# A hybrid decoder step on one core: the 16 learned rows moved into the sequences' tile, and 320 instead of 336 rows behind the keys

## The chip, the cores and the metric

The kernel runs on 1 core of one Trainium2 chip. The metric is the device time of one execution in microseconds. An execution was also profiled: its trace gives each instruction's engine, source line, start and duration. Engines are written as the profile writes them: PE is TensorE's matmul, PEld its weight load, DVE is VectorE, ACT is ScalarE, POOL is GpSimd, SP is SyncE; L723 is line 723 of the kernel.

## The reference

One layer is computed for two kinds of sequences: a prompt of 256 rows, ahead of which 16 learned rows stand (272 positions), and 8 running sequences with 8 new rows each (64 rows) and 1024 cached positions. Width is 1024, all in fp32.

```python
u = rmsnorm(h, norm1_g) @ w_in
z, xbc, dt_raw, q, k, v, f_raw, gate_s, gate_a = split(u)
xbc = silu(causal_dwconv(concat(conv_prev, xbc), conv_w, conv_b))      # width 4
y, ssm_state = ssm_run(xs, dt, A, Bm, Cm)                              # chunks: 16 learned rows, then 128 and 128
y = grouped_rmsnorm((y + d_skip * xs) * silu(z), ssd_norm_g)
o = attn_run(q, k, v, logf)              # causal; logit = q.k / 8 + c_q - c_k, c the running sum of log forget
mix = sigmoid(gate_s) * (y @ w_ssd_br) + sigmoid(gate_a) * (o @ w_attn_br)
h = h + mix @ w_out
h = h + hier_moe(rmsnorm(h, norm2_g))    # 4 groups x 8 experts, top 1 group, top 2 experts in it
y_prompt = rmsnorm(hp, final_norm_g)[:, 16:]
```

Returned are the outputs of the 256 prompt rows and of the 64 sample rows, the keys, values and log forget values of all 272 and 64 rows, the state-space states and the last convolution rows. The outputs of the 16 learned rows are not returned; their keys, values, log forget values, convolution rows and their part of the state are needed by the rows behind them.

## The kernel before

The 336 rows lie in three tiles, `ROWS = [128, 128, 80]`, beginning at columns 0, 128 and 256 of the transposed activations `xnT`. Tile 0 holds the 16 learned rows and prompt rows 0 to 111, tile 1 prompt rows 112 to 239, and tile 2 (80 rows) the 64 sample rows and then prompt rows 240 to 255. Each fp32 matmul shows as two records in the trace. The phases follow one another; each is a block with one instruction stream for each engine, and ends in a barrier.

*Setup.* The rows are normed and transposed, keys, values, time steps and forget values of all 336 rows are computed, and running sums are taken as products with triangular matrices (`tri_le`, `tri_le2` for tile 2, `ones` and `tailrow` for totals); `c_q` and `ncT` are those of log forget. POOL writes the masks `mask_d` (128 x 256) and `mask_t` (for the last 16 query rows).

*State-space phase.* Eight groups of 4 heads. For each, PE projects 512 channels over all 336 columns (`channels`, L667, 64 records), ACT and VectorE do the convolution and SiLU, then `chunks` does the rest: z gates (L676), transposes to rows (L688), decay products (L698), transposes of the old states (L709), products of states (L718), outputs inside a chunk (L723), outputs from the incoming state (L727, L733, L736), and new states of the samples (L751). Then PE goes on with the channels of the next group, as soon as VectorE has added up the first half of the samples' states (L645), which frees the PSUM banks. The order on VectorE behind the products of states is fixed by the program: copy of the first state L608, then decay (L611) and sum (L615) for the second and third; then the output rows of tile 0, 1, 2 (L621 to L631); then the prompt's state out (L637), and the samples' states (L639, L645). Tile 0 starts from a zero state, so it has two operations (L621, L631), while tiles 1 and 2 have four (L623, L627, L629, L631). POOL scales x by time step, end decay and skip for tile 0, 1, 2 (L503, three products each), and then spreads B over the samples (L506). The product of states of a tile waits for POOL's products of that tile:

```python
for t, r in enumerate(ROWS):
    pe.wait_ge(x_ok, 3 * g + t + 1)
    k0 = 64 if t == 2 else 0
    o = ps[7][:, 256 * t:256 * t + 256] if t < 2 else ps[3][:, 0:256]
    pe.matmul(o, tok[k0:r, t, 256:384], xw[k0:r, t, :], start=True, stop=True).then_inc(st_ps, 1)
```

*Attention, prompt.* Eight passes, each for a pair of heads. `scores` (L1103) has three products a head, for query tiles of 128, 128 and 16 rows over 128, 256 and 336 keys; then PE computes q of the next pair over all 336 columns (`project_q`, L1091, 16 records), while VectorE adds decay and mask (L1020), takes maxima (L1025), and after ScalarE's exponentials (L945) the reciprocal (L1031) and the scaling (L1036). Then PE transposes the weights (L1110 to L1115, six a head), ScalarE copies them out (L949, L950), and PE multiplies with v (L1122). The weights of q have one buffer `w_q`: POOL issues the two transfers for the next pair in `load_wq` (L868) once the projection that reads them is done (`q_ps`).

*Attention, samples*: one sequence after another over cached pages.

*Merge.* Eight column tiles: two gates (L1344), the state-space branch (L1349) and the attention branch (L1352), 40 products of 336 columns each; then the output product row tile by row tile (L1360), norm, transposes and router.

*Route, experts, final.* Each of the 336 rows chooses two experts; the pairs are counted into blocks of 64 rows, each block of one expert. For each block SP streams 6 MB of weights (`w_gate_up` in three buffers, `w_down` in two), PE gathers the rows with a 0/1 product over the three row tiles (L1700), and the block is computed (L1722, L1737). In the end the rows' two results are gathered, added and normed, and sent.

## Time and profile before

| what | value |
|---|---|
| runs of the kernel | 1520.16, 1515.48, 1518.97 us, median 1518.97 |
| profiled execution | 1519.67 us, its span 1518.0 us, mean granted clock 0.932 of 2.4 GHz |
| PE / PEld busy | 1338.1 us (88%) / 740.9 us (49%) |
| DVE / ACT / POOL busy | 493.4 us (32%) / 263.9 us (17%) / 207.1 us (14%) |
| setup | 0 to 78 us |
| state-space phase | 78 to 482 us |
| attention, prompt (loop of eight pairs) | 482 to 602 us (from 495) |
| attention, samples | 602 to 733 us |
| merge, output product and router | 733 to 919 us, 919 to 979 us |
| route | 979 to 1000 us |
| experts | 1000 to 1489 us |
| final | 1489 to 1518 us |

The stages' limits are read from the first and last instruction of their lines. A share of busy time is an average over stages with different limits: PE's 88% has the experts' phase in it, where DMA runs at 0.94. In an order of time each row has start (us), duration (us; of several merged instructions from the first start to the last end), engine, line, operation, tiles and count, and in brackets how long the engine stood idle before it and what ended that.

### The profile page before, as it was taken

The numbers are of one execution on the slowest core, as the hardware profiler recorded it, in microseconds if no ns is written. First come the engines' busy times: TensorE is split into PE (matmuls) and PEld (weight loads), VectorE is DVE, ScalarE is ACT, GpSimd is POOL, SyncE is SP. The second block draws the span as 40 slices with busy tenths as digits, with TensorE's granted clock in tenths as the row PEclk, the third lists the DMA queues.
The fourth block names the chain that finished last, engine by engine and source line by source line (L and its number), as shares of the span: only waits on it lengthen the run. The fifth ranks groups of instructions, "written<-read, shape, count | busy, mean of one in ns | idle before, by whom it ended". The sixth has DMA issues, their size and how long they took to land. (4 is left out here: it accounts for less than half of the span.)

```text
span 1518.0 us, 19560 instructions
## 1 busy us (share of the span) xinstructions
PE 1338.1 (88%) x6097; PEld 740.9 (49%) x6097; DVE 493.4 (32%) x1106; ACT 263.9 (17%) x677; POOL 207.1 (14%) x401
## 2 busy tenths in 40 slices
PE   5899999999995898877799999669999999999990
PEld 3666667666763455645566664423333333333330
DVE  2236654556456465333000001331221212122123
ACT  1122233223322344222000000001010111101011
POOL 3023443244324111010000000100000000000003
PEclk9789999989997898999899999779999999999995
DMA  6033324422422227543865370169999999999974
GB/s 195 19 111 88 113 83 142 114 86 83 142 59 58 45 52 250 176 149 104 247 145 120 87 235 0 69 284 421 429 428 429 429 429 429 429 428 429 428 295 128
DMA packets 171554, 318.30 MB, mean 210 GB/s; under 512 B 21147, under 2 KB 148563, under 8 KB 159235
## 3 DMA queue, kind: packets, MB, share of 16 engines
q1 hardware_dynamic: 162610, 302.03, 54.8%
q10 hardware_dynamic: 6864, 8.94, 1.7%
q0 software_dynamic: 2048, 6.95, 1.6%
q8 instruction: 16, 0.26, 0.1%
q14 instruction: 16, 0.12, 0.0%
HBM read 289.20 MB, written 28.68 MB: 209 GB/s over the span
## 5 line engine op out<-in xcount | busy, mean ns | idle before, releaser
L667 PE MATMUL psg<-stretch 128*128 128x336 f32 x512 | 162.3, 482 | 11.3 <-DVE h_sample_out L645 9.6
L1722 PE MATMUL ph<-w_gate_up,x_gathered 128*64 128x512 f32 x704 | 162.2, 612 | 0.9 <-DVE x_gathered L1670 0.9
L667 PEld LDWEIGHTS psg<-stretch 128*128 128x128 f32 x512 | 105.0, 207 | 70.4 <-DVE h_sample_out L645 15.4
L1737 PE MATMUL py<-w_down,h_t 128*64 128x512 f32 x512 | 116.9, 598 | 3.5 <-DMA w_down<-in_w_exp_down 3.4
L1682 DVE SCALAR_TENSOR_TENSOR h_gate<-h_tanh,ph 128x256 f32<-128x256 f32 x32 | 13.5, 421 | 301.0 <-ACT h_tanh L1639 301.0
L1722 PEld LDWEIGHTS ph<-w_gate_up,x_gathered 128*64 128x64 f32 x704 | 49.4, 135 | 108.5 <-issue 108.5
L1700 PE MATMUL px<-yT,block_rows 128*64 128x512 f32 (+1 forms) x396 | 92.9, 605 | 10.7 <-DVE block_rows L1665 10.7
L582 DVE SCALAR_TENSOR_TENSOR x_conv<-x_padded,conv_wh,x_conv 128x360 f32<-128x360 f32 x96 | 57.0, 594 | 103.5 <-ACT x_conv L531 92.6
L676 PE MATMUL psg<-stretch 128*128 128x256 f32 (+1 forms) x384 | 84.5, 380 | 0.0
L1344 PE MATMUL psm<-stretch,w_merge 128*128 128x336 f32 x256 | 76.2, 457 | 6.9 <-DMA w_merge<-in_w_in 6.9
L1774 POOL DMA_INDIRECT y_expert<-expert_rows,slot_i x6 | 6.2, 1041 | 510.2 <-PEq L1744 508.7
L676 PEld LDWEIGHTS psg<-stretch 128*128 128x128 f32 (+1 forms) x384 | 67.3, 177 | 14.5
L1722 PE MATMUL ph<-stretch,x_gathered 128*64 128x512 f32 x320 | 73.9, 612 | 0.0
L1349 PE MATMUL psm<-yT,w_merge 128*128 128x336 f32 x256 | 73.6, 446 | 0.0
L1344 PEld LDWEIGHTS psm<-stretch,w_merge 128*128 128x128 f32 x256 | 49.9, 196 | 31.7 <-issue 9.0
L1304 DVE SCALAR_TENSOR_TENSOR mix_part<-gate_tanh,psm 128x336 f32<-128x336 f32 x16 | 7.4, 501 | 178.5 <-PE psm L1352 178.5
L1737 PEld LDWEIGHTS py<-w_down,h_t 128*64 128x64 f32 x512 | 33.9, 136 | 64.2 <-issue 58.9
L1700 PEld LDWEIGHTS px<-yT,block_rows 128*64 128x64 f32 (+1 forms) x396 | 28.3, 139 | 70.0 <-issue 59.2
L1349 PEld LDWEIGHTS psm<-yT,w_merge 128*128 128x128 f32 x256 | 48.6, 190 | 23.7
L1091 PE MATMUL psa<-stretch,w_q 128*128 128x336 f32 x128 | 42.3, 488 | 16.1 <-DVE k_and_c L1000 12.6
L1639 ACT ACTIVATE h_tanh<-ph 128x256 f32<-128x256 f32 x32 | 12.3, 384 | 211.4 <-PE ph L1722 211.4
L1722 PEld LDWEIGHTS ph<-stretch,x_gathered 128*64 128x64 f32 x320 | 22.4, 135 | 49.3 <-issue 49.3
(414 smaller groups left out, 1791.1 us busy)
## 6 DMA issues: line engine op xcount, KB each, us to landing
w_down<-in_w_exp_down SPq DMA_DIRECT2D x32, 2048.0 KB, 19.6
w_gate_up<-in_w_exp_gate SPq DMA_DIRECT2D x22, 2048.0 KB, 17.0
w_gate_up<-in_w_exp_up SPq DMA_DIRECT2D x22, 2048.0 KB, 21.4
stretch<-in_w_exp_gate SPq DMA_DIRECT2D x10, 2048.0 KB, 18.7
stretch<-in_w_exp_up SPq DMA_DIRECT2D x10, 2048.0 KB, 23.1
stretch<-in_w_in SPq DMA_DIRECT2D x16, 1024.0 KB, 5.1
stretch<-in_w_in SPq DMA_DIRECT2D x16, 512.0 KB, 7.4
h<-in_state_ssm SPq DMA_DIRECT2D x16, 512.0 KB, 4.9
```

What stands on the lines that cost most here:

```text
L582: i = v.scalar_tensor_tensor(xc[:, m, :], xp[:, m, w:w + 360], S["conv_wh"][:, w, bass.ds(o, 1)], xc[:, m, :], ALU.mult, ALU.add)
L667: mm = pe.matmul(ps[m][:, 0:T], wg[:, k, P * m:P * m + P], S["xnT"][:, k, :], start=(k == 0), stop=(k == KT - 1))
L676: mm = pe.matmul(ps[4 + t // 2][0:r, 256 * (t % 2):256 * (t % 2) + 256], S["xnT"][:, k, COL[t]:COL[t] + r], wg[:, k, 512:768], start=(k == ...
L1091: mm = pe.matmul(ps[0][:, 0:T], wq[:, k, :, :], S["xnT"][:, k, :], start=(k == 0), stop=(k == KT - 1))
L1304: k = v.scalar_tensor_tensor(mx_[h][:, j, :], th[h][:, j, :], 1.0, ps[4 * h + 2 + j][:, 0:T], ALU.add, ALU.mult)
L1344: mm = pe.matmul(ps[4 * h + j][:, 0:T], wm[h][:, 8 * j + k, :], S["xnT"][:, k, :], start=(k == 0), stop=(k == KT - 1))
L1349: pe.matmul(ps[4 * h + 2][:, 0:T], wm[h][:, 16 + k, :], S["yT"][:, k, :], start=(k == 0), stop=(k == 15))
L1639: act.activation(th[:, :], ph[:, 0:256], ACT.Tanh, scale=0.5).then_inc(th_ok, 1)
L1682: v.scalar_tensor_tensor(hg[:, :], th[:, :], 1.0, ph[:, 0:256], ALU.add, ALU.mult).then_inc(gu_free, 1)
L1700: mm = pe.matmul(px[64 * j:64 * j + 64, :], sel[0:r, t, :], S["hn"][0:r, t, 512 * j:512 * j + 512], start=(t == 0), stop=(t == 2))
L1722: mm = pe.matmul(ph[64 * j:64 * j + 64, :], xg[:, k % 4, k // 4, :], w_gu[w][:, :, k, :].rearrange("p g (q c) -> p g q c", c=4)[:, :, :, 2 ...
L1737: mm = pe.matmul(py[h][64 * j:64 * j + 64, :], ht[:, k % 2, k // 2, :], w_dn[h][:, k, 512 * j:512 * j + 512], start=(k == 0), stop=(k == 3))
```

## The change

The learned rows move from the front of tile 0 to the end of tile 2 (columns 320 to 335). Tiles 0 and 1 now hold the 256 prompt rows, and tile 2 the 64 sample rows and the 16 learned rows. What needs all 336 rows (norm, channels, keys, values, time steps, running sums, states) runs as before on `ROWS`; what only the returned outputs need runs on `QROWS = [128, 128, 64]` and `TQ = 320` columns: z gates, y, q, gates, branches, output product, norm, router, experts and final norm. The first chunk of the scan is now the 16 rows of tile 2, and tiles 0 and 1 both start from a state. Keys are laid out with the 16 learned ones first (`k_and_c`, 272 columns), so there are two query tiles with 144 and 272 keys, and the learned rows' v is copied to `v_meta`. The numbers of expert blocks that the program provides for (`NBLK` 42, `LEAST_BLK` 10) come out as before; one of the five comparisons that count an expert's blocks falls away. The diff, cut to its core:

```diff
+TQ = SEQ + NS
+QROWS = [128, 128, 64]
-            sp.dma_start(S["xtok"][0:16, 0, :], A["meta_tokens"]).then_inc(x_in, 16)
-            sp.dma_start(S["xtok"][16:128, 0, :], xp[0:112, :]).then_inc(x_in, 16)
-            sp.dma_start(S["xtok"][:, 1, :], xp[112:240, :]).then_inc(x_in, 16)
+            sp.dma_start(S["xtok"][:, 0, :], xp[0:128, :]).then_inc(x_in, 16)
+            sp.dma_start(S["xtok"][:, 1, :], xp[128:256, :]).then_inc(x_in, 16)
...
-            sp.dma_start(S["xtok"][64:80, 2, :], xp[240:256, :]).then_inc(x_in, 16)
+            sp.dma_start(S["xtok"][64:80, 2, :], A["meta_tokens"]).then_inc(x_in, 16)
...
-            pool.memset(S["mask_t"][:, :], 0.0)
             pool.drain()
-            keep(S["mask_d"][:, 128:256], [[-1, P]], 0, 1, fill=NEG)
-            pool.memset(S["mask_t"][:, 256:320], NEG)
-            keep(S["mask_t"][:, 320:336], [[-1, 16]], 0, 1, fill=NEG)
+            keep(S["mask_d"][:, 144:272], [[-1, P]], 0, 1, fill=NEG)
...
-            pe.matmul(o[:, 128:144], S["tri_le"][:, :], lf[:, 0, :], start=True, stop=True)
-            pe.matmul(o[:, 144:160], S["ones"][:, :], lf[:, 0, :], start=True, stop=False)
+            pe.matmul(o[:, 128:144], S["tailrow"][:, :], lf[0:80, 2, :], start=True, stop=False)
+            pe.matmul(o[:, 128:144], S["tri_le"][:, :], lf[:, 0, :], start=False, stop=True)
+            pe.matmul(o[:, 144:160], S["tailrow"][:, :], lf[0:80, 2, :], start=True, stop=False)
+            pe.matmul(o[:, 144:160], S["ones"][:, :], lf[:, 0, :], start=False, stop=False)
             pe.matmul(o[:, 144:160], S["tri_le"][:, :], lf[:, 1, :], start=False, stop=True)
-            pe.matmul(o[0:16, 160:176], S["ones"][:, 0:16], lf[:, 0, :], start=True, stop=False)
-            pe.matmul(o[0:16, 160:176], S["ones"][:, 0:16], lf[:, 1, :], start=False, stop=False)
-            pe.matmul(o[0:16, 160:176], S["tri_le2"][:, 64:80], lf[0:80, 2, :], start=False, stop=True)
...
-                for t, r in enumerate(ROWS):
-                    v.wait_ge(y_ps, 3 * g + t + 1)
-                    if t == 0:
-                        v.tensor_tensor(y[0:r, t, :], ps[4 + t][0:r, 0:256], dx[0:r, t, :], ALU.add)
-                    else:
-                        v.tensor_tensor(yo[0:r, t, :].rearrange("k (h p) -> k h p", h=4),
...
+                for t, r in enumerate(QROWS):
+                    v.wait_ge(y_ps, 3 * g + t + 1)
+                    v.tensor_tensor(yo[0:r, t, :].rearrange("k (h p) -> k h p", h=4),
+                                    ps[4 + t][0:r, 256:512].rearrange("k (h p) -> k h p", h=4),
+                                    bc(S["eac"][0:r, t, bass.ds(4 * g, 4)].unsqueeze(2), [r, 4, HP]), ALU.mult)
+                    v.drain()
+                    v.tensor_tensor(y[0:r, t, :], ps[4 + t][0:r, 0:256], yo[0:r, t, :], ALU.add)
+                    v.drain()
+                    v.tensor_tensor(y[0:r, t, :], y[0:r, t, :], dx[0:r, t, :], ALU.add)
...
-                for t, r in enumerate(ROWS):
-                    pe.wait_ge(x_ok, 3 * g + t + 1)
-                    k0 = 64 if t == 2 else 0
-                    o = ps[7][:, 256 * t:256 * t + 256] if t < 2 else ps[3][:, 0:256]
-                    pe.matmul(o, tok[k0:r, t, 256:384], xw[k0:r, t, :], start=True, stop=True).then_inc(st_ps, 1)
+                pe.wait_ge(x_ok, 3 * g + 3)
+                for t in (2, 0, 1):
+                    k = slice(64, 80) if t == 2 else slice(0, P)
+                    o = (ps[7][:, 256:512], ps[3][:, 0:256], ps[7][:, 0:256])[t]
+                    pe.matmul(o, tok[k, t, 256:384], xw[k, t, :], start=True, stop=True).then_inc(st_ps, 1)
...
-                    if t == 1:
-                        pe.wait_ge(hp_ok, 3 * g + 1)
-                        mm = pe.matmul(ps[5][:, 256:512], xs[:, 3, P:2 * P], hp[:, 0, :], start=True, stop=True)
+                    if t < 2:
+                        pe.wait_ge(hp_ok, 3 * g + t + 1)
+                        mm = pe.matmul(ps[4 + t][:, 256:512], xs[:, 3, 16 + P * t:16 + P * t + P], hp[:, t, :],
+                                       start=True, stop=True)
                     if t == 2:
                         pe.wait_ge(compact, 2 * g + 2)
-                        pe.wait_ge(hp_ok, 3 * g + 2)
                         pe.wait_ge(ht_ev, 4 * g + 4)
-                        pe.matmul(ps[6][64:80, 256:512], cx[:, 8, 64:80], hp[:, 1, :], start=True, stop=True)
...
-        keys = [128, 256, T]
-        qrows = [128, 128, TAIL]
+        keys = [144, 272]
...
-                    for c in range(3):
-                        k = 3 * g2 + c
-                        r = qrows[c]
-                        act.wait_ge(nm_ok, 6 * t + k + 1)
+                    for c in range(2):
+                        k = 2 * g2 + c
+                        act.wait_ge(nm_ok, 4 * t + k + 1)
...
-                    act.activation(pt[:, g2, 0:416], ps[5 + 2 * g2][:, 0:416], ACT.Copy)
-                    act.activation(pt[0:80, g2, 416:432], ps[5 + 2 * g2][0:80, 416:432], ACT.Copy).then_inc(pt_ev, 1)
+                    act.activation(pt[:, g2, :], ps[5 + 2 * g2][:, 0:384], ACT.Copy)
+                    act.activation(ptm[:, g2, :], ps[2 + 2 * g2][0:16, 0:256], ACT.Copy).then_inc(pt_ev, 1)
...
-                    mm = pe.matmul(ps[0][:, 0:T], wq[:, k, :, :], S["xnT"][:, k, :], start=(k == 0),
+                    mm = pe.matmul(ps[0][:, 0:TQ], wq[:, k, :, :], S["xnT"][:, k, 0:TQ], start=(k == 0),
...
+                    for c in range(2):
+                        pe.transpose(bm_[0:16, P * c:P * c + P], sc[:, g2, c, 0:16], idn[:, :])
+                        pe.transpose(b[:, P * c:P * c + P], sc[:, g2, c, 16:144], idn[:, :])
+                    pe.transpose(b[:, 256:384], sc[:, g2, 1, 144:272], idn[:, :]).then_inc(pt_ps, 1)
...
+                for g2 in range(2):
+                    pe.matmul(ps[6][64 * g2:64 * g2 + 64, 0:256], S["v"][:, 0, P * u + HD * g2:P * u + HD * g2 + HD],
+                              pt[:, g2, 0:256], start=True, stop=False)
+                for g2 in range(2):
+                    pe.matmul(ps[6][64 * g2:64 * g2 + 64, 128:256], S["v"][:, 1, P * u + HD * g2:P * u + HD * g2 + HD],
+                              pt[:, g2, 256:384], start=False, stop=False)
+                for g2 in range(2):
+                    mm = pe.matmul(ps[6][64 * g2:64 * g2 + 64, 0:256],
+                                   vm[:, P * u + HD * g2:P * u + HD * g2 + HD], ptm[:, g2, :],
+                                   start=False, stop=True)
...
-                            mm = pe.matmul(ps[4 * h + j][:, 0:T], wm[h][:, 8 * j + k, :], S["xnT"][:, k, :],
+                            mm = pe.matmul(ps[4 * h + j][:, 0:TQ], wm[h][:, 8 * j + k, :], S["xnT"][:, k, 0:TQ],
...
-                for t, r in enumerate(ROWS):
+                for t, r in enumerate(QROWS):
```

The last pair of lines stands for all the loops over row tiles from the z gates on.

## Rows read from the trace of the kernel before

**Rows 1.** Busy us by stage: PE, PEld, DVE, ACT, POOL; PEclk, DMA share, GB/s.
```profile
...
78.00:482.00 404.00, 381.26 (x1725) 263.62 (x1726) 219.91 (x376) 118.00 (x304) 145.20 (x283) 0.94 0.34 98
...
495.00:602.00 107.00, 92.45 (x416) 54.28 (x416) 63.11 (x225) 43.71 (x158) 17.64 (x20) 0.91 0.38 103
...
733.00:919.00 186.00, 183.56 (x640) 122.90 (x640) 11.38 (x24) 7.22 (x16) 0.00 (x0) 0.98 0.62 164
...
1000.00:1489.00 489.00, 469.13 (x2128) 157.94 (x2128) 95.88 (x228) 51.12 (x97) 0.00 (x0) 0.99 0.94 399
```

**Rows 2.** Order of time, tail of one state-space group: start, duration, engine, line.
```profile
...
262.78 1.03 PE L718 MATMUL psg<-x_wend,x_b_rows 128*128 128x256 f32 x4
...
263.84 0.42 DVE L608 COPY h_prompt<-psg 128x256 f32<-128x256 f32 x1 [0.79 <-PE psg L718]
...
264.47 0.48 DVE L611 TENSOR_TENSOR h_prompt<-h_prompt,dec 128x256 f32<-128x256 f32 x1 [0.20 <-issue]
264.63 2.07 POOL L506 TENSOR_TENSOR b_by_seq<-x_b_rows,seg 64x1024 f32<-64x1024 f32 x1
...
264.71 0.69 PE L718 MATMUL psg<-x_wend,x_b_rows 16*128 16x256 f32 x2 [0.91 <-POOL x_skip L503]
...
265.64 1.34 DVE L611 TENSOR_TENSOR h_prompt<-h_prompt,dec 128x256 f32<-128x256 f32 x1 [0.20 <-PE psg L718]
...
267.56 0.42 DVE L621 TENSOR_TENSOR y_rows<-psg,x_skip 128x256 f32<-128x256 f32 x1
...
268.41 0.42 DVE L623 TENSOR_TENSOR y_off<-psg,eac 128x256 f32<-128x256 f32 x1
...
272.21 0.41 DVE L637 COPY h_prompt_out<-psg 128x256 f32<-128x256 f32 x1
...
275.17 1.49 PE L667 MATMUL psg<-stretch 128*128 128x336 f32 x2 [1.37 <-DVE h_sample_out L645]
```

**Rows 3.** Order of time in the attention loop: one middle pair, the sixth, the last.
```profile
...
516.79 1.75 POOL L868 DMA_DIRECT2D w_q<-in_w_in  x2 [11.67 <-PE psa L1091]
...
519.34 2.44 PE L1103 MATMUL psa<-k_and_c,q_pad 128*128 128x128 f32 x10
...
522.38 4.79 PE L1091 MATMUL psa<-stretch,w_q 128*128 128x336 f32 x16
...
527.00 0.27 PE L1110 MATMUL psa_s<-ident,scores 128*128 128x128 f32 x1
...
580.96 2.25 PE L1091 MATMUL psa<-stretch,w_q 128*128 128x336 f32 x7 [0.63 <-DMA w_q<-in_w_in]
...
596.58 0.47 PE L1110 MATMUL psa_s<-ident,scores 128*128 128x128 f32 x1 [4.29 <-DVE scores L1036]
```

**Rows 4.** Order of time on PE, two ends of another group.
```profile
...
311.39 1.03 PE L718 MATMUL psg<-x_wend,x_b_rows 128*128 128x256 f32 x4
...
326.61 21.35 PE L667 MATMUL psg<-stretch 128*128 128x336 f32 x64 [1.37 <-DVE h_sample_out L645]
```

**Rows 5.** Windows of 6 us, columns as in rows 1; PEclk is the granted clock.
```profile
...
214.00:220.00 6.00, 5.75 (x36) 4.50 (x38) 5.21 (x10) 0.51 (x2) 3.19 (x4) 0.72 0.00 0
...
274.00:280.00 6.00, 4.83 (x12) 3.18 (x13) 5.70 (x8) 0.00 (x0) 4.85 (x8) 0.72 0.00 0
...
316.00:322.00 6.00, 6.00 (x31) 3.27 (x30) 2.85 (x8) 1.02 (x4) 1.48 (x4) 0.50 0.00 0
```

**Rows 6.** Groups of instructions by line and shape, the third query tile on VectorE.
```profile
...
L1025 DVE TENSOR_REDUCE neg_max<-scores 16x1 f32<-16x336 f32 x16 | 7.7, 480 | 0.0
...
L1036 DVE TENSOR_SCALAR scores<-scores,row_sum 16x336 f32<-16x336 f32 x16 | 6.0, 376 | 0.0
...
L1020 DVE SCALAR_TENSOR_TENSOR scores<-psa_s,c_q,mask_t 16x336 f32<-16x336 f32 x8 | 4.4, 546 | 0.0
```

**Rows 7.** DMA issues of the attention stage: KB each, median us to landing.
```profile
...
w_q<-in_w_in POOLq DMA_DIRECT2D x16, 256.0 KB, 4.0
```

**Rows 8.** Order of time in setup, one pair of wide products.
```profile
...
71.82 0.59 PE L350 MATMUL ps<-lf,tri_le 128*128 128x16 f32 x2
```

240 lines of the change are left out of this document (107 added, 133 removed).

## The prediction

> **What bounds the kernel now.** I read the busy time by stage first [rows 1]. The stages follow one another, each ended by a barrier, so a stage that shortens or lengthens moves all that follows. The last long one, the experts, keeps the DMA engines at 0.94 of their time while it streams weights: its length is that of its bytes, and fewer rows shorten it only if a 64-row block disappears. The routing worked out from the reference's inputs gives each of the 32 experts 10 to 33 pairs with the 16 learned rows and 10 to 31 without them. So there are 32 blocks before and 32 after, and the stage keeps its length; a block less would have been worth about 6 MB at 399 GB/s, 16 us. That leaves the three stages before it, and each has its own bound.
>
> In the state-space stage TensorE is busy 381 of 404 us. The order of time in one of the eight groups [rows 2] shows where it isn't: it waits 0.91 us for POOL's products of the third tile (L718), and 1.37 us at the head of the next group's L667 for VectorE's L645. From L608 to L645 VectorE runs almost without a hole, and TensorE's wait hangs on its end. Whatever lengthens that chain lengthens the group.
>
> In the prompt's attention the order of time of one head pair [rows 3] shows scores (L1103), then the next pair's q projection (L1091), then the transposes (L1110) as soon as the projection ends: TensorE goes from one to the next, and VectorE's softmax lies beneath the projection. Only the last pair has no projection, and there L1110 waits 4.29 us for VectorE.
>
> In the merge TensorE is busy 183.6 of 186 us with 640 records of 336 columns [rows 1].
>
> **The change part by part.**
>
> *Merge.* All 640 records go from 336 to 320 columns. In proportion that is 183.6 x 16/336 = 8.7 us off a stage in which nothing else waits. The output product, the transposes and the router behind it stream the same number of columns: nothing.
>
> *State-space stage, the waits.* The first product of states is now that of the learned rows, which lie in the third tile, so all three L718 pairs wait for POOL's last product. The first of them starts at 264.71 instead of 262.78. The 16-row pair lasts until 265.34 (the next line's start is taken as that: 264.71 plus 0.63, an estimate from the pair's 0.69); the pair behind it ends 0.6 later, the four records' 1.03 less two steps of 0.21. VectorE's copy L608 then starts near 265.97, not at 263.84: 2.13 later. Some comes back: the second L611 took 1.34 against 0.48 for the first, beside POOL's L506 (264.63 plus 2.07 is 266.70, and the long one ends 0.28 after that). Started 2 us later, both multiplications fall at or behind 266.6: 0.86 back.
>
> *State-space stage, the work.* The first tile gets the term of the starting state: two VectorE instructions and a product more. The first tile's two operations take 268.41 - 267.56 = 0.85, the two other tiles' four each take 272.21 - 268.41 = 3.80, 1.90 a tile. Three tiles of four are 5.70 against 4.65: 1.05 more. TensorE's added product lies beneath this chain, as does the one taken out (L733) and POOL's saved copy; the 80-row operations that become 64-row ones have as many elements per partition and cost the same.
> Together 2.13 - 0.86 + 1.05 = 2.3 us a group, 8 groups, 18.6 us. Bounds: 1.05 x 8 = 8.4 if the later start were hidden, (2.13 + 1.05) x 8 = 25.4 if nothing comes back.
>
> *State-space stage, the clock.* TensorE's wait at L718 grows from 0.91 us to about 1.8, the one at L667 from 1.37 to 3.7. After the 1.37 us wait the granted clock falls in each group (0.72 in the mean of 274 to 280 us [rows 5], a mix of the levels 1.2 and 2.4 GHz), so nothing new there. After the 0.91 us it falls in three of seven groups: to 0.72 in the mean in two, the first of which is shown, and to 0.50 throughout in the third [rows 5]. From L718 to the next L667 a group without the fall takes 275.17 - 262.78 = 12.39 us [rows 2], the third one 326.61 - 311.39 = 15.22 [rows 4], 2.83 more; the two shorter falls I put at 1.6 each by their half as long stay at the lower level, an estimate. At 1.8 us I take it to fall in all eight, five more; VectorE's longer chain covers a part, so 1.0 each: 5 us. Bounds: 0, and 5 x 2.83 = 14.
> By the Trainium skill ("TensorE: Matmul & The Clock Gate", section "HAM oscillation — how this bites in real kernels") gaps that come round in each pass make the engine pay the return to half speed in each of them; that speaks against this change, and is the second rival below. The trace agrees at the 1.37 us wait and, at 0.91 us, in three groups of seven.
>
> *Attention.* VectorE loses the third query tile: for each head 546 + 480 + 376 ns [rows 6], 2.8 us a pair. That is not what the pair gains. On TensorE the scores go from 720 to 416 columns a head, 3.04 us (519.34 to 522.38) to 1.76; the projection loses 16/336 of 4.62 (522.38 to 527.00), 0.22; transposes and copies lose perhaps 0.35 (five transposes of six); the product with v streams 640 columns a head in place of 432, by the scores' rate (3.04 for 1440) and with the two heads side by side 0.45 more. The projection could so start 1.28 + 0.35 - 0.45 = 1.2 earlier, but its weights come through one buffer: POOL issues them when the last projection is done, at 516.79, the second issue starts 0.88 later and lands 4.0 after that [rows 7], at 521.7, and the projection runs at 522.38. So 0.7 can be had, not 1.2; with 0.22 that is 0.9 a pair. Five of the middle pairs get it, 4.5 us. The sixth already waits for its weights (580.96, 0.63 [rows 3]) among the cache pages: nothing. In the last pair VectorE's 2.7 comes out whole. The first pair and the smaller tiles to clear: 0.6, an estimate. Sum 7.8 us. Bounds: 3.3 (last pair and start alone) and 8 x 2.8 = 22.4.
>
> *The rest.* In setup the sums of the log forget values have wide products in place of narrow ones; a pair takes 0.59 [rows 8], about one pair and a third more, less the mask writes that POOL no longer does: 0.3 more (bounds -0.5 and 0.8). Routing has four comparisons of block counts instead of five, on VectorE's own chain: 0.3 less, an estimate below the 0.42 of a wider operation (L608 [rows 2]). One DMA issue less at each end is taken at nothing: others of the same size land beside it. The sample's attention keeps its work.
>
> **Sum.** 18.6 + 5 + 0.3 - 8.7 - 7.8 - 0.3 = +7.1 us on the profiled execution's own 1519.67 (0.70 above the median of the runs): 1526.8, told as 1527.
>
> **The rivals.**
> 1. *As summed*: 1527, chance 0.46. The likeliest case's own range is 1520 to 1534.
> 2. *The clock falls in the tail of every group, and long*: all eight at 2.83 are 22.6, less the 6.0 that the three cost now (2.83 + 2 x 1.6): 16.6 in place of 5, 1538. For it: the waits double. Against: while TensorE is at half speed VectorE is still the one waited for. Chance 0.14. This is what the skill's rule named above would give.
> 3. *Evens out*: no further falls, and the weights of q land early enough for the 1.4 us (1.2 and 0.22) a pair: 1527 - 5 - 2.5 = 1519.5. For it: the 0.91 us wait left the clock alone in four groups. Against: the wait is now longer than the one that always made it fall. Chance 0.22.
> 4. *Faster: VectorE is the bound of the attention loop*, and the 2.8 us it loses come out in all eight pairs: 22.4 in place of 7.8, 1512. It decides once a pair gains 2.4 us, since then 8 x 2.4 = 19.2 outweighs the rest by more than 4 us. For it: VectorE is busy 63 of 107 us there [rows 1], in a chain with ScalarE. Against: in the middle pairs L1110 follows the end of L1091 (its records 522.38 plus 4.79) without a wait for VectorE [rows 3]. Chance 0.13.
> What is left, 0.05, is something not seen.
>
> **How the numbers follow.** A measurement of this kernel tells a change of about 0.3%, 4.6 us: 1514.4 to 1523.5 is no change. A fifth of case 1 lies in there, four fifths above. Slower: 0.37 + 0.14 + 0.03 + half of the unseen, 0.56; same: 0.09 + 0.17 + a little, 0.28; faster: 0.13 + 0.02 and the rest, 0.16. The range takes case 1 with its bounds, case 3, the upper half of case 4 and most of case 2: 1513 to 1540.
>
> **What would show it.** In the profile after: L667's wait for VectorE's last sum should be 3.5 to 4 us in place of 1.37, with the group's period some 2.3 us longer; all L718 should wait for POOL about 1.8 us; the granted clock should fall behind it in nearly every group. The merge stage should be 177 to 178 us. In the attention loop L1091 should wait for the w_q transfer in the middle pairs, and the pair should be near 10.4 us. The expert stage should be 489 us, with 32 gate tiles. The forecast is wrong if L667's wait stays below 2 us (the chain doesn't set the group), or if the attention loop loses over 15 us (case 4).

## The result, and the profile after

The changed kernel takes 1537.34 us in the median of four executions (1535.26 to 1539.63), the kernel before 1517.22 in the median of its four: a ratio of 1.0139 [1.0115, 1.0162]. It is slower, by 20 us where 7 were forecast (1527 against a profiled 1519.67), near the upper end of the range. The profiled executions, 1519.67 and 1537.96, differ by 18.3, and so do their spans.

Where the 18.3 us lie shows in the stages, each taken from the first TensorE instruction of one to that of the next:

| stage | before | after | change | forecast |
|---|---|---|---|---|
| setup, to the first channels | 77.78 | 80.91 | +3.1 | +0.3 |
| state-space, to the first q projection | 417.56 | 450.96 | +33.4 | +23.6 |
| prompt's attention | 107.37 | 95.52 | -11.9 | -7.8 |
| samples' attention | 131.12 | 131.90 | +0.8 | 0 |
| merge | 185.36 | 176.69 | -8.7 | -8.7 |
| output product, router, routing | 81.30 | 80.65 | -0.6 | -0.3 |
| experts and end | 517.51 | 519.67 | +2.2 | 0 |

The windows by stage of the changed kernel, columns as in [rows 1]:

```profile
81.00:518.00 437.00, 405.24 (x1727) 275.44 (x1727) 212.31 (x392) 118.18 (x304) 143.08 (x275) 0.91 0.32 91
532.00:627.00 95.00, 74.63 (x368) 48.87 (x368) 41.91 (x144) 36.21 (x120) 17.66 (x20) 0.95 0.31 71
759.00:936.00 177.00, 174.95 (x641) 122.95 (x641) 11.01 (x24) 7.01 (x16) 0.00 (x0) 0.99 0.65 172
1016.00:1507.00 491.00, 474.47 (x2128) 155.10 (x2128) 95.83 (x228) 51.12 (x97) 0.00 (x0) 0.99 0.94 398
```

The merge is as forecast. The state-space stage has the same number of TensorE records within two, but 405 us of them where there were 381, at a granted clock of 0.91 in place of 0.94. In the experts TensorE is busy 5.3 us more, with the same 2128 records in a window 2 us longer: TensorE works longer on each block, which the forecast didn't have; whether the stage is longer for it is taken up behind the experiments.

The tail of one group of the changed kernel, in order of time; it answers to [rows 2]:

```profile
280.19 1.89 POOL L499 TENSOR_TENSOR b_by_seq<-x_b_rows,seg 64x1024 f32<-64x1024 f32 x1
...
280.37 1.73 PE L708 MATMUL psg<-x_wend,x_b_rows 16*128 16x256 f32 x6 [1.87 <-POOL x_skip L496]
...
281.70 0.42 DVE L600 COPY h_prompt<-psg 128x256 f32<-128x256 f32 x1 [3.09 <-PE psg L708]
...
282.32 0.43 DVE L603 TENSOR_TENSOR h_prompt<-h_prompt,dec 128x256 f32<-128x256 f32 x1 [0.20 <-PE psg L708]
...
284.54 0.42 DVE L613 TENSOR_TENSOR y_off<-psg,eac 128x256 f32<-128x256 f32 x1 [0.18 <-issue]
...
290.02 0.41 DVE L627 COPY h_prompt_out<-psg 128x256 f32<-128x256 f32 x1
...
290.49 1.12 PE L740 MATMUL psg<-b_by_seq,x_wend 32*128 32x512 f32 x2 [1.05 <-DVE h_prompt_out L627]
...
292.98 3.61 PE L657 MATMUL psg<-stretch 128*128 128x336 f32 x6 [1.37 <-DVE h_sample_out L635]
```

The forecast's steps can be followed from the start of the transposes of the old states, 276.58 here (L699) and 261.03 before (L709). VectorE's copy of the first state (L600) comes 5.12 after it where it came 2.81 after, 2.31 later (forecast 2.13); the multiplications L603 take 0.43 again, not 1.34; the first tile's y has its two more instructions; and the next group begins 16.40 after in place of 14.14: 2.26 later, forecast 2.3. This part was right. But the group as a whole grew by 3.1, from 48.87 to 51.98 where the clock doesn't fall. The other 0.8 lies ahead of this tail, in TensorE's weight loads, first of the changed kernel and then of the kernel before:

```profile
261.18 0.40 PEld L747 LDWEIGHTS psg<-ident,y_rows 64*128 64x128 f32 x3 [0.17 <-issue]
...
261.75 0.14 PEld L747 LDWEIGHTS psg<-ident,y_rows 64*128 64x128 f32 x1 [0.17 <-issue]
...
269.06 3.21 PEld L666 LDWEIGHTS psg<-stretch 128*64 128x64 f32 x16 [0.33 <-issue]
...
272.66 0.64 PEld L678 LDWEIGHTS psg<-ident,x_silu 128*128 128x128 f32 x6 [0.38 <-issue]
```
```profile
245.89 0.83 PEld L758 LDWEIGHTS psg<-ident,y_rows 128*128 128x128 f32 x6
246.69 10.19 PEld L676 LDWEIGHTS psg<-stretch 128*128 128x128 f32 x48
256.94 0.79 PEld L688 LDWEIGHTS psg<-ident,x_silu 128*128 128x128 f32 x6
```

These are the transposes of y (64 rows now, 80 before) and z's third tile (weights of 64 columns, 80 before), both between instructions on the full 128 x 128. At each passage from one size to the other the weight load stands idle for 0.17 to 0.38 us. Before, the 80-row loads are merged into the rows of the 128-row ones, since no such gap parts them. From the channels' start to z's start the group takes 20.96 us in place of 20.46, from z's start to the next transposes 10.70 in place of 10.40. The prediction had this at nothing.

The attention loop, one middle pair, and setup's first product of running sums, which answer to [rows 3] and [rows 8]:

```profile
567.49 4.57 PE L1075 MATMUL psa<-stretch,w_q 128*128 128x320 f32 x16 [0.96 <-DMA w_q<-in_w_in]
```
```profile
73.93 0.59 PE L345 MATMUL ps<-lf,tailrow 80*128 80x16 f32 x2
```

L1075 waits 0.72 to 0.96 for its weights in the six middle pairs, which take 10.4 to 10.6: as forecast.

### The profile page after: what moved, and what is told of

Same layout as the page of the kernel before. It is cut to its first block and busy times, and to the rows that moved or that the text cites. A ratio compares the mean times of both kernels' runs of the same rounds, so it can differ in the third digit from the quotient of the medians.

```text
span 1536.3 us, 19335 instructions
## 1 busy us (share of the span) xinstructions
PE 1339.0 (87%) x6047; PEld 741.9 (48%) x6047; DVE 464.9 (30%) x1049; ACT 256.3 (17%) x637; POOL 203.9 (13%) x390
## 5 line engine op out<-in xcount | busy, mean ns | idle before, releaser
L657 PE MATMUL psg<-stretch 128*128 128x336 f32 x512 | 162.4, 483 | 9.4 <-DVE h_sample_out L635 7.7
L657 PEld LDWEIGHTS psg<-stretch 128*128 128x128 f32 x512 | 105.2, 207 | 70.0 <-DVE h_sample_out L635 15.0
L1686 PE MATMUL px<-yT,block_rows 128*64 128x512 f32 (+1 forms) x396 | 97.1, 609 | 10.4 <-DVE block_rows L1651 10.4
L1330 PE MATMUL psm<-stretch,w_merge 128*128 128x320 f32 x256 | 72.7, 443 | 7.2 <-DMA w_merge<-in_w_in 7.2
L666 PEld LDWEIGHTS psg<-stretch 128*128 128x128 f32 (+1 forms) x384 | 64.9, 172 | 18.3 <-issue 2.7
L1335 PE MATMUL psm<-yT,w_merge 128*128 128x320 f32 x256 | 70.2, 432 | 0.0
L1686 PEld LDWEIGHTS px<-yT,block_rows 128*64 128x64 f32 (+1 forms) x396 | 25.0, 135 | 77.7 <-issue 67.2
L1075 PE MATMUL psa<-stretch,w_q 128*128 128x320 f32 x128 | 40.1, 470 | 22.3 <-DVE k_and_c L988 13.6
L1290 DVE SCALAR_TENSOR_TENSOR mix_part<-gate_tanh,psm 128x320 f32<-128x320 f32 x16 | 7.1, 484 | 170.6 <-PE psm L1338 170.6
## 6 DMA issues: line engine op xcount, KB each, us to landing
w_down<-in_w_exp_down SPq DMA_DIRECT2D x32, 2048.0 KB, 18.3
w_gate_up<-in_w_exp_up SPq DMA_DIRECT2D x22, 2048.0 KB, 20.4
stretch<-in_w_exp_up SPq DMA_DIRECT2D x10, 2048.0 KB, 21.8
```

The source lines that it names most:

```text
L657: mm = pe.matmul(ps[m][:, 0:T], wg[:, k, P * m:P * m + P], S["xnT"][:, k, :], start=(k == 0), stop=(k == KT - 1))
L666: mm = pe.matmul(ps[4 + t // 2][0:r, 256 * (t % 2):256 * (t % 2) + 256], S["xnT"][:, k, COL[t]:COL[t] + r], wg[:, k, 512:768], start=(k == ...
L1075: mm = pe.matmul(ps[0][:, 0:TQ], wq[:, k, :, :], S["xnT"][:, k, 0:TQ], start=(k == 0), stop=(k == KT - 1))
L1290: k = v.scalar_tensor_tensor(mx_[h][:, j, :], th[h][:, j, :], 1.0, ps[4 * h + 2 + j][:, 0:TQ], ALU.add, ALU.mult)
L1330: mm = pe.matmul(ps[4 * h + j][:, 0:TQ], wm[h][:, 8 * j + k, :], S["xnT"][:, k, 0:TQ], start=(k == 0), stop=(k == KT - 1))
L1335: pe.matmul(ps[4 * h + 2][:, 0:TQ], wm[h][:, 16 + k, :], S["yT"][:, k, :], start=(k == 0), stop=(k == 15))
```

## The experiments

Of each kernel's profiled execution, the stretches of a group (us; the value that comes most often) and the tails, from the first product of states to the next group's start. Seven of the eight tails end in a next group.

| kernel | channels to z | z to transposes | transposes to states | tail, full clock | tails that the clock lengthens |
|---|---|---|---|---|---|
| before | 20.46 | 10.40 | 5.62 | 12.39 | 3 (13.99, 14.00, 15.22) |
| changed | 20.96 | 10.70 | 7.71 | 12.61 | 4 (14.96 to 16.25) |
| changed, parameters first | 20.96 | 10.70 | 7.71 | 12.61 | 4 (14.96 to 16.31) |
| 80 rows, three places | 20.46 | 10.40 | 7.65 | 12.62 | 0 |
| 80 rows, z alone | 20.96 | 10.46 | 7.65 | 12.63 | 4 (14.97 to 16.60) |
| 80 rows, y alone | 20.46 | 10.64 | 7.71 | 12.62 | 2 (14.97, 14.98) |
| changed, x_wend first | 20.7 to 22.3 | 10.70 | 5.77 | 14.32 | 0 |
| before, later start | 20.46 or 21.5 | 10.40 | 7.66 | 11.48 | 3 (16.3) |
| before, more VectorE | 21.8 | 10.40 | 5.62 | 13.35 | 0 |
| combination | 21.7 | 10.40 | 5.71 | 13.37 | 0 |
| before, POOL's order | 20.2 to 21.8 | 10.40 | 5.62 | 11.84 | 0 |
| combination, VectorE's order | 18.77 or 20.46 | 10.40 | 5.71 | 10.27 | 0 |
| before, both orders | 18.77 | 10.40 | 5.62 | 9.93 | 0 |
| the combination on 64 rows | 19.27 or 20.9 | 10.70 | 5.77 | 10.27 | 0 |

### 80 rows again in three places

```diff
             pool.memset(hp[:, 0, :], 0.0)
+            pool.drain()
+            pool.memset(y[64:80, 2, :], 0.0)
...
                 pe.wait_ge(wz_in, 16 * g + 16)
-                for t, r in enumerate(QROWS):
+                for t, r in enumerate(ROWS):
...
                 for h in range(2):
-                    for t, r in enumerate(QROWS):
+                    for t, r in enumerate(ROWS):
                         mm = pe.transpose(ps[6 + h][:, COL[t]:COL[t] + r], y[0:r, t, P * h:P * h + P],
...
+            v.memset(S["hn"][64:80, 2, :], 0.0)
...
                 pe.wait_ge(sel_ok, n)
-                for t, r in enumerate(QROWS):
+                for t, r in enumerate(ROWS):
```

The three loops are z's, the transposes of y and the experts' gather.

> The changed kernel with the third tile's matmuls on 80 rows again in three places (gates z, transposes of y, gather of the experts); the 16 added rows are zeros or go unread, the other engines keep 64 rows. Theory (a matmul with 64 rows or columns of weights beside ones of 128 makes TensorE wait before its weights are loaded): per group the channels' start to z's start goes back from 20.96 to 20.46 us, z's start to the token transposes from 10.70 to 10.40, and two gathers stand 14.75 us apart in place of 14.86. That is 8 x 0.8 + 32 x 0.11 = 9.9 us, so about 1527.5 beside 1537.3. Rival (the 0.5 us is the one wait for all three tiles of y, the 0.3 us something of z's, the experts' 2.4 us DMA): those stretches stay as in the changed kernel, 1537.

Measured: 1516.0 us, 1.0015 [0.9992, 1.0039] of the kernel before on that chip (1514.83). The stretches went back as expected (20.46 and 10.40; two gathers mostly 14.72 apart, where the changed kernel has 14.86), but the time expected, 1527.5, was missed by 11 us. In the profiled executions the state-space stage is 20.4 us shorter than in the changed kernel: 6.4 ahead of the tails and 13.0 in them, since no tail loses the clock here. (The ten executions lie between 1513.22 and 1529.19, and one of them is profiled.) The edit has a price of its own, too: the zeros that it writes into `hn` take VectorE 0.91 us, and the output product, router and routing are 2.0 us longer than in the changed kernel. The third tile's gather in the changed kernel and in this one, TensorE's weight loads:

```profile
1227.39 0.19 PEld L1686 LDWEIGHTS px<-yT,block_rows 64*64 64x64 f32 x4 [0.81 <-issue]
```
```profile
1205.37 0.15 PEld L1689 LDWEIGHTS px<-yT,block_rows 80*64 80x64 f32 x2 [0.28 <-issue]
```

With 80 rows the loads follow at the pace of all the others, with 64 the first one waits for the products ahead of it. The granted clock in windows of 6 us over a tail (columns as in [rows 5]), two of the changed kernel, then two of this one:

```profile
226.00:232.00 6.00, 5.98 (x26) 5.18 (x27) 3.69 (x9) 0.00 (x0) 1.73 (x1) 0.69 0.00 0
232.00:238.00 6.00, 6.00 (x33) 3.08 (x31) 3.38 (x9) 1.02 (x4) 1.48 (x4) 0.74 0.00 0
```
```profile
223.00:229.00 6.00, 6.00 (x50) 4.58 (x48) 4.61 (x12) 0.51 (x2) 0.86 (x2) 1.00 0.00 0
229.00:235.00 6.00, 3.57 (x12) 1.30 (x11) 5.62 (x11) 1.02 (x4) 3.92 (x7) 1.00 0.00 0
```

TensorE waits 1.87 us for POOL ahead of the products of states in both, in all eight groups. In this profile the wait is thus not enough for the fall, and the edit that takes the short stalls away takes the falls away. That the stalls are needed for a fall isn't shown by it: the next section has a kernel with the same wait, no 64-row weights, and three falls.

Which of the two stalls of a group does it, asked with z alone and y alone on 80 rows:

> The changed kernel with z's third tile alone on 80 rows (weights 128x80 in place of 128x64). The kernel with 80 rows in all three places lost no tail to the clock, where the changed kernel loses five; this and the next run ask which of the two short stalls of a group brings the falls. In both cases z's start to the token transposes goes from 10.70 to 10.40, 2.4 us in all. If z's stall brings the falls: no long tails, some 13 us more, near 1522. If that of y's transposes brings them: the tails fall as before, near 1535.

> The changed kernel with y's transposes alone on 80 rows (weights 80x128 in place of 64x128). In both cases the channels' start to z's start goes from 20.96 to 20.46, 4 us in all. If this stall brings the clock's falls in the tails: none of them, some 13 us more, near 1520. If z's brings them: near 1533. If either alone is enough to bring them, both this run and the one of z's stay above 1530.

Measured: 1525.19 us for z (1.0060 [1.0038, 1.0083]), 1524.23 for y (1.0080 [1.0046, 1.0114]; its executions lie between 1521.91 and 1537.37). Neither is all of it: each takes back its own stretch (z's to 0.06 us), four tails fall in the one profile and two in the other, and of these profiles only the one with 80 rows in all three places has none. Why the clock falls in one tail and not in the next of the same kernel isn't settled by this.

### The later start alone, and the added work alone

Both are edits of the kernel before. The products of states first:

```diff
                 for t, r in enumerate(ROWS):
-                    pe.wait_ge(x_ok, 3 * g + t + 1)
+                    pe.wait_ge(x_ok, 3 * g + 3)
```

> The kernel before with one edit: its products of states all wait for POOL's third tile, in the order of before. This is the later start alone, without the added work of VectorE. Theory: 2.1 us later less 0.9 that comes back, 1.2 us a group or 10 us, and falls of the clock as in the changed kernel (five tails in place of three), up to 7 us more: 1527 to 1534. Rival (the start alone costs nothing, since VectorE or the next group's weights set the end): 1517 to 1520.

Then the first tile's y:

```diff
                     if t == 0:
+                        v.tensor_tensor(yo[0:r, t, :].rearrange("k (h p) -> k h p", h=4),
+                                        ps[4 + t][0:r, 0:256].rearrange("k (h p) -> k h p", h=4),
+                                        bc(S["eac"][0:r, t, bass.ds(4 * g, 4)].unsqueeze(2), [r, 4, HP]), ALU.mult)
+                        v.drain()
+                        v.tensor_tensor(yo[0:r, t, :], ps[4 + t][0:r, 0:256], yo[0:r, t, :], ALU.add)
+                        v.drain()
                         v.tensor_tensor(y[0:r, t, :], ps[4 + t][0:r, 0:256], dx[0:r, t, :], ALU.add)
```

> The kernel before with two more VectorE instructions in the first tile's y, of the size of the changed kernel's (a product with a broadcast factor and an addition, into a scratch tile that nobody reads). This is the added work alone, without the later start. Theory: the copy of the prompt's state and the head of the next group come 1.05 us later in each group, 8.4 us, and up to 7 us more where tails fall that did not: 1523 to 1531 beside 1515. Rival (the work lies beneath TensorE): 1514 to 1517.

Measured: 1536.54 us (1.0131 [1.0103, 1.0158]) and 1527.34 (1.0094 [1.0066, 1.0121]). The steps of the prediction stand: transposes to states 2.04 more and the tail 0.91 less make 1.13 a group for the later start (forecast 2.13 - 0.86 = 1.27), and the tail with the added work is 0.96 longer (forecast 1.05). Together that is 2.1, the changed kernel's 2.3. The clock then goes two ways. With the later start, slower than the 1527 to 1534 expected, the state-space stage is 26.8 us longer than in the profile before (444.3 for 417.6), and the steps make 9.0 of it: three tails last 16.3 (a granted clock of 0.50 in the window below, the lower level of 1.2 GHz), and most heads 21.2 to 21.6. TensorE waits 1.87 us for POOL in all eight groups of this kernel, and it has no weights of 64 rows or columns in this stage. With the added work the stage is 7.1 longer (424.7), and the steps alone make 7.7: no tail falls, the clock stays low in the head of each next group, 21.8 us from channels to z in place of 20.46, and its mean over the stage is the same 0.92 as before (0.88 with the later start). By the medians this kernel loses 15.6 us (1527.34 and 1511.70), though the profiled execution of the kernel before took 1519.67. The two windows are of the first kernel's tail and of the second one's head:

```profile
230.00:234.00 4.00, 4.00 (x23) 2.79 (x24) 1.70 (x4) 0.75 (x4) 0.74 (x2) 0.50 0.00 0
```
```profile
278.50:284.00 5.50, 5.50 (x10) 3.49 (x11) 4.52 (x6) 0.00 (x0) 3.68 (x7) 0.50 0.02 4
```

### Setup

```diff
 sp.dma_start(S["xtok"][64:80, 2, :], A["meta_tokens"]).then_inc(x_in, 16)
+sp.wait_ge(par_in, 160)
 sp.dma_start(w_dt[:, :, :], win[:, :, C_DT:C_DT + 32]).then_inc(w_in_ready, 16)
```

> The changed kernel with one more wait in setup: the weights of dt, k and v are requested only when the small parameter rows have landed. Theory (one DMA less ahead of them lets the 2 MB of weights go out in front of the last parameter rows, which land at 16.4 us in place of 13.6, and TensorE's first instruction waits for them): the parameters land before 10 us, the transposes of x start at 13 to 15 us in place of 18.3, and the first group begins 2 to 4 us earlier, at 77 to 79 in place of 80.9; 1533 to 1535. Rival (the landing time is chance, or the weights then land too late): the first group begins at 80 us or later, 1537 or more.

Measured: 1534.87 us (1.0130 [1.0110, 1.0151]), the first group at 78.78. ACT's first use of the last parameter row, in the kernel before, the changed one and this one:

```profile
13.65 0.23 ACT L200 ACTIVATE a_neg<-brow 128x32 f32<-128x32 f32 x1 [1.29 <-DMA brow<-in_b_forget]
```
```profile
16.36 0.23 ACT L196 ACTIVATE a_neg<-brow 128x32 f32<-128x32 f32 x1 [4.40 <-DMA brow<-in_b_forget]
```
```profile
11.91 0.23 ACT L197 ACTIVATE a_neg<-brow 128x32 f32<-128x32 f32 x1
```

It isn't chance: in the five profiles with the requests of before it comes at 13.2 to 14.1, in the five with the changed ones at 16.1 to 16.5, and with the weights held back at 11.7 to 11.9 in four. That the weights of k and v take the DMA engines ahead of the parameter rows because they are requested 0.5 us earlier is a reading of this; the order of the row transfers ahead of them changed as well, and wasn't tried alone. The transposes of x, which begin 5.2 us earlier with the wait, are then held 2.78 us by VectorE, so that 2.1 is left of it. The other 1.0 of setup's 3.1 is the sums: 14.33 us from the first decay sums to the transposes of k before, 15.34 after, where 0.3 was forecast.

### POOL's order

```diff
-                for t, r in enumerate(ROWS):
-                    pool.wait_ge(tok_ev, 3 * g + t + 1)
...
+                for n, (dst, by) in enumerate(((xw, S["w_end"]), (xdt, S["dt"]), (dx, S["dskip"][:, :].unsqueeze(1)))):
+                    for t, r in enumerate(ROWS):
+                        if n == 0:
+                            pool.wait_ge(tok_ev, 3 * g + t + 1)
...
+                                           bc(f.unsqueeze(2), [r, 4, HP]), ALU.mult).then_inc(x_ok, 1)
...
-                pe.wait_ge(x_ok, 3 * g + 3)
+                pe.wait_ge(x_ok, 9 * g + 3)
...
                     pe.wait_ge(m_ok, 3 * g + t + 1)
+                    pe.wait_ge(x_ok, 9 * g + t + 4)
...
                     v.wait_ge(y_ps, 3 * g + t + 1)
+                    v.wait_ge(x_ok, 9 * g + t + 7)
```

> The changed kernel with POOL's nine products of a group in another order: the three x_wend first, then the three x_dt, then the three x_skip, each with a count of its own, so that the products of states wait for the three x_wend alone. Theory (the later first product of states costs 2.1 us a group and the clock's falls): the wait of 1.87 us is gone, VectorE's copy of the first state starts some 1.9 us earlier, 0.9 of it lost again beside POOL's products; 1.0 to 2.0 us a group, 8 to 16 us, and up to 7 us more if the clock's falls in the tails go from five groups to none. 1515 to 1529, 1520 the middle. Rival (VectorE's longer chain is the loss, and the wait lies beneath it): under 4 us, 1533 or more.

Measured: 1521.73 us (1.0044 [1.0026, 1.0063]). The time lies in the range expected, but not for the reason expected: the wait is gone (transposes to states 5.77), yet the tail grew by 1.7 and the group kept only 0.23; most of the gain is the clock, since no tail is longer by it. VectorE's multiplication by the decay is the place:

```profile
272.05 1.89 POOL L498 TENSOR_TENSOR b_by_seq<-x_b_rows,seg 64x1024 f32<-64x1024 f32 x1
...
272.23 1.99 DVE L602 TENSOR_TENSOR h_prompt<-h_prompt,dec 128x256 f32<-128x256 f32 x1 [0.19 <-PE psg L708]
274.29 0.42 DVE L606 TENSOR_TENSOR h_prompt<-h_prompt,psg 128x256 f32<-128x256 f32 x1
...
274.92 0.43 DVE L602 TENSOR_TENSOR h_prompt<-h_prompt,dec 128x256 f32<-128x256 f32 x1 [0.21 <-issue]
```

L602 reads two tiles from SBUF and ends 0.28 after POOL's product; the same instruction takes 0.43 when POOL's product is over. In the changed kernel's tail above, the copy L600, which reads PSUM, took its usual 0.42 beside the same POOL product (281.70). The Trainium skill ("GPSIMD Engine Reference", section "1. Specifications") says that GpSimd shares its SBUF interfaces with VectorE, in contention with instructions that have two SBUF inputs; the trace agrees, with 1.99 us beside POOL against 0.43. So in the next kernel b_by_seq went ahead of the x_skip products, together with the 80 rows and the order in setup; and the kernel before got the same POOL order alone:

```diff
+                    if n == 2:
+                        pool.tensor_tensor(bm[:, :, :], bc(tok[0:64, 2, 256:384].unsqueeze(1), [NS, NSEQ, N]),
+                                           bc(S["seg8"][:, :].unsqueeze(2), [NS, NSEQ, N]), ALU.mult).then_inc(b_ok, 1)
                     for t, r in enumerate(ROWS):
                         if n == 0:
```

> The changed kernel with 80 rows in the three places, the parameter rows ahead of the weights in setup, and POOL's order: three x_wend, three x_dt, then b_by_seq, then the three x_skip. In the run with the first order the copy of the first state came 1.9 us earlier, but VectorE's next multiplication took 1.99 us in place of 0.43, ending 0.28 after POOL's b_by_seq; with b_by_seq ahead of it the multiplication should take under 1.1. Theory (the start of the products of states sets the group's end): a group of 49.4 to 50.0 us in place of 51.13, 9 to 14 us less than with 80 rows alone, and 2 less in setup: 1500 to 1505 beside 1515 for the kernel before. Rival (another operation beside POOL is stretched instead): groups of 50.8 or more, 1511 to 1515.

> The kernel before with the same order on POOL. Theory: the wait of 0.91 us goes and the multiplication of 1.34 us takes 0.5: 0.9 us a group or 7 us, and up to 6 us from the three tails that fall: 1502 to 1508 beside 1515. Then the order is worth about as much without the change, and the change itself is worth nothing more than its gains outside the state-space stage. Rival (before has nothing to win there): 1513 to 1516.

Measured: 1513.23 us (0.9988 [0.9974, 1.0001]) and 1507.18 (0.9947 [0.9929, 0.9965]). The multiplication took 0.86, and the first group lasted 49.43, inside the expected 49.4 to 50.0. The others lasted 50.9 to 51.2: what the tail gained (1.2) the clock took in the head of the next group (21.7 in place of 20.46), so the expected time was missed by 8 us, and the rival's time came out, though no other operation beside POOL was stretched. In the kernel before the order brings what was expected, and there the changed rows stand 6 us behind. TensorE had nothing left to do in that tail; it waited for VectorE (1.79 and 1.37).

### VectorE's order

The two loops became functions of their bodies, `y_tile` (a tile's y) and `h_half` (half of the samples' states), called in another order; the line between the calls is as it was:

```diff
+                y_tile(0, QROWS[0])
...
                 v.tensor_copy(hpo[:, :, :], ps[3][:, 256:512].rearrange("p (a n) -> p a n", a=2)).then_inc(hf_ev, 1)
+                h_half(0)
+                y_tile(1, QROWS[1])
+                y_tile(2, QROWS[2])
+                h_half(1)
```

> The last combination (80 rows, parameters first, POOL's new order) with one more edit: VectorE makes the first tile's y, then the prompt's state and the first half of the samples' states, then the y of the two other tiles, then the second half. The next group's first product waits for that first half alone, so VectorE's longer y no longer lies ahead of it. Theory (VectorE's chain sets the group's end): the next group's start comes 2.5 to 3.5 us earlier and TensorE's long idle stretch in the tail goes, and with it the fall of the clock at the next group's head: groups of 46.9 to 48.5 us in place of 51.1, 1480 to 1494. Rival (the later y holds up POOL's work for the next group): groups of 50 or more, 1505 to 1513.

> The kernel before with POOL's new order and the same order on VectorE. Theory: its VectorE chain was 1.0 shorter, so it has less to win: groups of 46.7 to 47.6 us in place of 48.2, 1496 to 1503. If so, with VectorE's work off the path in both, the change is worth what it takes from the merge and the attention, less some 3 us of setup and of 16-row products: 8 to 16 us less in the changed kernel than here. Rival (the change costs TensorE more than that in each group): both within 5 us.

Measured: 1476.17 us, 0.9762 [0.9739, 0.9786] of the kernel before (1511.70 beside it), and 1484.42, 0.9820 [0.9797, 0.9844]. Both beat all kernels above, by more than expected. The end of a tail in the changed kernel with all orders:

```profile
256.99 1.99 PE L751 MATMUL psg<-b_by_seq,x_wend 32*128 32x512 f32 x8
260.15 2.54 PE L667 MATMUL psg<-stretch 128*128 128x336 f32 x5 [1.17 <-DVE h_sample_out L635]
```

The eight products of the samples' states run in one piece, VectorE's y of the tiles 1 and 2 lies beneath the next channels, and TensorE waits 1.17 once. In five groups of eight the clock then doesn't fall in the head either: 18.77 from channels to z, which no group but a first one of some kernels had before. With VectorE off the path the changed rows are 8.2 us better than those of before, the lower end of the expected 8 to 16. From the profiles: the attention 9.9 shorter, the merge 8.6; the state-space stage 7.9 longer (0.33 in the tail, three groups with a fall in place of one, the stage's end), the samples' attention 4.9 longer, which no edit touches (129.5 to 134.5 us in the fourteen profiles), the experts 2.1 shorter.

The last run put the third tile back on 64 rows in this kernel:

> The last combination of the changed kernel (POOL's and VectorE's new orders, parameters first) with the third tile's matmuls back on 64 rows in the three places. Theory (each place costs TensorE a stall of its own, whatever else sets the end): 0.8 us a group and 0.11 us an expert block more than with 80 rows, 9.9 us, 1486; with falls of the clock in the tails as well, up to 1500. Rival (the 64 rows cost only where the waits of before stand beside them): 1474 to 1479.

Measured: 1487.34 us (0.9806 [0.9785, 0.9826]). That is 11.2 more than with 80 rows, but on another chip, where the kernel before takes 1516.22 in place of 1511.70; by the two ratios it is 0.0044, 6.7 us. From channels to z 0.50 more, from z on 0.30, 6.4 us in eight groups: this cost stands by itself, without the long waits beside it. The two intervals leave the 6.7 uncertain by some 5 us, so this run doesn't tell 6.4 from the 9.9 expected with the expert blocks.

## Why the prediction was wrong in size

The failed step is this one: "the 80-row operations that become 64-row ones have as many elements per partition and cost the same". That holds for VectorE and ACT. On TensorE they cost 0.8 us in each group, 6.3 us in the stage, which the prediction put at nothing. And in this kernel the clock's falls in the tails hang on them: with 80 rows in three places the profiled execution has none, and the changed kernel takes 1516.0, the same as before within its interval. The Trainium skill ("TensorEngine Tiling (Array Packing)", section "Tiling Modes") has a rule for it that the prediction didn't weigh: to change between tiling modes, among which it counts 128 x 64, 64 x 128 and 64 x 64, drains TensorE. The runs agree, with 0.17 to 0.38 us a passage in the state-space stage, and none between 80 and 128; that the size alone puts a plain product into such a mode is a reading that no run here tests.

The 33.4 us of the state-space stage are 18.5 for the forecast's steps (forecast 18.6), 6.3 for the 64-row and 64-column weights (nothing), 7.1 for the clock (5), and 1.5 behind the last group (nothing), where TensorE waits 0.5 longer for VectorE's `y_rows` and 1.0 longer for its `k_and_c`.

Point by point:

- *Merge*: right, 8.7.
- *Waits and work of the state-space stage*: right, 2.3 a group (2.09 and 0.22), and each half shown by a run of its own. The sign that it named for this was wrong: the wait of the next group's first product for VectorE (L667 before, L657 after) stayed at 1.37, and the prediction had called itself wrong below 2. The chain does set the group; the wait only showed one instruction earlier, at the last products of the samples' states (1.05, at 290.49 above, where it was 0.16), since the second wait spans only the two VectorE instructions behind those products. Before:

```profile
272.68 1.12 PE L751 MATMUL psg<-b_by_seq,x_wend 32*128 32x512 f32 x2 [0.16 <-DVE h_prompt_out L637]
```

- *Clock*: forecast 5 more falls at 1.0. The tails cost 13.0 in place of 6.0 in the profiles (five of eight fall in place of three, the eighth seen in its products alone), 7.0. That the size is near is luck, for the reason given, the longer wait, doesn't decide. All eight groups wait 1.87 us in the changed kernel, in the one with 80 rows and in the kernel before with the later start, and of their eight tails five, none and four fall (the eighth seen in its products alone). The last of these kernels has no 64-row weights in the stage, so they don't decide alone either; what does stays open. The rival at 1538 lies closest to the time, but not all eight groups fall, and most of the loss isn't clock.
- *Attention*: 11.9 for 7.8. The pair is as forecast, with the wait for w_q, and the rival of VectorE as the bound falls. Too low were the sixth pair (1.5 where nothing was forecast: it goes from 11.96 to 10.41, and its wait for w_q lasts 0.77), the last pair (3.3 for 2.7), the start (1.5 for 0.6) and one pair of before that had run slower (12.85 in place of 11.25).
- *Experts*: 32 blocks, and the length is that of the bytes, both as forecast. Two gathers stand 14.86 us apart with 64 rows and 14.72 with 80, but in the middle of the stage the DMA moves the same in both, and at the end TensorE waits for it: the last seven gathers of the kernel before come 15.1 to 15.4 us behind the one ahead of them, the last two of the changed one 15.1 and 15.3. Windows and waits, before and after:

```profile
1245.00:1345.00 100.00, 98.14 (x450) 33.15 (x448) 20.70 (x49) 10.45 (x20) 0.00 (x0) 1.00 1.01 429
...
1464.73 3.65 PE L1737 MATMUL py<-w_down,h_t 128*64 128x512 f32 x16 [0.45 <-DMA w_down<-in_w_exp_down]
```
```profile
1260.00:1360.00 100.00, 98.43 (x448) 32.17 (x446) 19.05 (x47) 10.46 (x20) 0.00 (x0) 1.00 1.01 428
...
1483.07 3.65 PE L1723 MATMUL py<-w_down,h_t 128*64 128x512 f32 x16 [0.37 <-DMA w_down<-in_w_exp_down]
```

  From the first gather to the end, the eight profiles with 80 rows in the gather take 517.5 to 520.3 us and the six with 64 rows 519.1 to 521.1. The 2.2 us lie within that spread; by the means the 64 rows cost 1.0 us, where 32 times 0.14 would be 4.5.
- *Setup*: 3.1 for 0.3. "One DMA issue less at each end is taken at nothing" failed: with the changed requests the rows that TensorE's first instruction waits for come 2.7 us later, and with the 2 MB of weights held back they come before 12 us. The other 1.0 is the sums.

In sum (33.4 - 23.6) + (3.1 - 0.3) + 2.2 + 0.8 - 4.1 - 0.3 = 11.2, the 18.3 less the 7.1 forecast. The 2.2 of the experts and the 0.8 of the samples' attention are no more than such profiles differ by.

## What to carry to other kernels

Cost a change of a tile's rows on each engine by itself: on TensorE a third tile of 64 rows between tiles of 128 was dearer than one of 80 with 16 idle rows, and where the clock falls in some passes of a loop, such stalls can cost more than their own length (here 6.3 us by themselves, and 13.0 in the tails of the one profile against none in the other). A wait that moves from one instruction to another on the same engine isn't gone: add the idle time up over the group. And when one engine's chain sets a loop's end, look for the part that the next pass doesn't need: moving two tiles' y behind the states on VectorE was worth more here (34 us by the two ratios, 19 in the kernel before) than the whole change. And where two engines run close together, as TensorE and the DMA do in the experts, time that one of them loses needn't lengthen the stage.

## What was not expected of the hardware

- Weights of 64 rows or 64 columns among full ones: 0.17 to 0.38 us of idle weight load at each passage; of 80, none.
- The granted clock changed in places far from the edits. The kernel before returned to the full level late in the head of each group (0.72 over 6 us, [rows 5]); with both orders it didn't fall there in five to seven groups of eight, 1.7 us a group; with 1 us more of VectorE in the tail it fell for 5.5 us at 0.50. Which stretch decides isn't settled here.
